# A two-block transformer kernel on one core: first stream in pieces, product quarters ahead of attention's first macro, a finer wait in the state-space output, one ones matmul for each norm

## What is computed

```python
h = x
h = h + nsa_mixer(rmsnorm(h), ...)      # 16 heads: compressed, selected and window attention, gated
h = h + s5_mixer(rmsnorm(h), ...)       # state space, GLU with gelu, output product
h = rmsnorm(h, final_norm)
h = h + even_mixer(rmsnorm(h), ...)     # stick-breaking attention beside retention
h = h + conv_ffn(rmsnorm(h), ...)
h = h + odd_mixer(rmsnorm(h), ...)      # gated linear attention, gates from log_sigmoid, chunks of 64
h = h + conv_ffn(rmsnorm(h), ...)
```

## Time and profile before

| | |
|---|---|
| median of 3 runs | 1942.9 us (1942.57 to 1943.28) |
| the profiled execution | 1942.15 us, its span 1940.3 us |
| PE busy | 1916.4 us, 99% of the span |
| DVE, ACT, POOL busy | 1144.0, 578.4 and 795.3 us |
| the chain that ended last, by engine | PE 89%, DVE 8%, waits for nothing visible 1%, ACT 1%, DMA 1% |
| DMA | 167.72 MB, mean 86 GB/s |
| TensorE clock granted, mean | 0.997 |

### The profile page before, as it was taken

How to read it: one execution, slowest core, us unless ns; L and a number is a source line. 1 busy time by engine, 2 the same in 40 slices (tenths; PEclk the granted TensorE clock), 3 DMA queues, 4 the chain that set the end, 5 groups by cost and what they waited for, 6 DMA issues and landing times.

```text
span 1940.3 us, 26524 instructions
## 1 busy us (share of the span) xinstructions
PE 1916.4 (99%) x9866; PEld 1517.6 (78%) x9866; DVE 1144.0 (59%) x2079; ACT 578.4 (30%) x1118; POOL 795.3 (41%) x454
## 2 busy tenths in 40 slices
PE   8999999999999999999999999999999999999999
PEld 5967777788788776777688888888788888888887
DVE  5769998788975545766664444333654454445311
ACT  3126566416641134454221111101322221111000
POOL 3532222368754432222244444444233334444443
PEclk9999999999999999999999999999999999999999
DMA  5621111223123231121132222232112222222332
GB/s 185 186 76 34 44 34 34 77 84 112 34 68 102 92 125 55 55 66 65 61 109 97 97 97 97 98 109 98 65 66 77 76 99 92 95 96 97 110 118 76
DMA packets 54628, 167.72 MB, mean 86 GB/s; under 512 B 6864, under 2 KB 14928, under 8 KB 54144
## 3 DMA queue, kind: packets, MB, share of 16 engines
q1 hardware_dynamic: 46624, 155.21, 23.8%
q10 hardware_dynamic: 7904, 11.16, 2.1%
HBM read 157.96 MB, written 2.10 MB: 82 GB/s over the span
## 4 chain that ended last, share of the span: by engine, by line
PE 89%; DVE 8%; issue 1%; ACT 1%; DMA 1%; ACTq 0%; POOL 0%; DVEq 0%
PE bank L186 18%; PE bank L187 17%; PE bank L190 17%; PE bank L587 5%; PE bank L592 5%; PE bank L588 5%; DVE prob L1656 2%; DVE ssb L1643 2%; PE bank L1278 1%; PE bank L200 1%; PE bank L206 1%; PE bank L1303 1%; PE bank L203 1%; PE bank L2634 1%; PE bank L2623 1%
## 5 line engine op out<-in xcount | busy, mean ns | idle before, releaser
L169 POOL TENSOR_TENSOR wlo<-raw,whi 128x1024 fp32r<-128x1024 f32 x248 | 594.8, 2398 | 895.5 <-DVE whi L177 895.5
L177 DVE CAST whi<-raw 128x1024 fp32r<-128x1024 f32 x288 | 206.4, 717 | 338.4 <-PE bank L190 240.9
L186 PE MATMUL bank<-xh,whi 128*128 128x512 f32 x888 | 347.1, 391 | 0.0
L187 PE MATMUL bank<-xl,whi 128*128 128x512 f32 x888 | 345.6, 389 | 0.0
L190 PE MATMUL bank<-xh,wlo 128*128 128x512 f32 x888 | 219.4, 389 | 0.0
L186 PEld LDWEIGHTS bank<-xh,whi 128*128 128x128 f32 x888 | 166.7, 188 | 37.6 <-issue 3.1
L187 PEld LDWEIGHTS bank<-xl,whi 128*128 128x128 f32 x888 | 166.7, 188 | 34.9 <-issue 0.5
L190 PEld LDWEIGHTS bank<-xh,wlo 128*128 128x128 f32 x888 | 166.7, 188 | 34.7
L587 PE MATMUL bank<-xh,whi 128*128 128x512 f32 x424 | 175.3, 414 | 1.4 <-DVE whi L177 1.4
L588 PE MATMUL bank<-xl,whi 128*128 128x512 f32 x424 | 166.0, 392 | 0.0
L186 PE MATMUL bank<-ghi,whi 128*128 128x512 f32 x308 | 119.8, 389 | 0.0
(11 more groups left out here) (431 smaller groups left out, 3477.6 us busy)
## 6 DMA issues: line engine op xcount, KB each, us to landing
raw<-in_weights_dram SPq DMA_DIRECT2D x288, 512.0 KB, 3.2
h<-in_x_dram SPq DMA_DIRECT2D x2, 1024.0 KB, 7.2
out_dram<-h ACTq DMA_DIRECT2D x8, 256.0 KB, 2.0
etab<-in_even_tables_dram ACTq DMA_DIRECT2D x1, 1730.0 KB, 6.5
sz<-su SPq DMA_DIRECT2D x16, 64.0 KB, 2.0
sz<-su SPq DMA_DIRECT2D x16, 48.0 KB, 2.0
x_kh<-kvc_h ACTq DMA_DIRECT2D x2, 256.0 KB, 5.0
x_kl<-kvc_l ACTq DMA_DIRECT2D x2, 256.0 KB, 6.9
```

The costliest lines, as they stand in the source:

```text
L169: nc.gpsimd.tensor_tensor(wlo[:, s % 2, :], raw[:, s, :], whi[:, s % 2, :].bitcast(F32), ALU.subtract).then_inc(w_lo, 1)
L177: nc.vector.tensor_copy(whi[:, t_of_4 % 2, :], raw[:, t_of_4, :]).then_inc(w_hi, 1)
L186: nc.tensor.matmul(to, w_h[k], rhs_hi(k), start=first and k == 0, stop=False)
L187: nc.tensor.matmul(to, w_h[k], rhs_lo(k), start=False, stop=False)
```

## The change

Six edits. (1) At the start SP asks for `x` in four pieces of two chunks, with the first weight tile between the second and the third, and takes over `nsa_loads` from ACT. ACT issues the gains first, then `wgate`, `tables` and `par`; it starts on the first pieces when gains and piece are there, and its waits for `tables` stand where they are first used. PE runs three instead of four matmuls on zeros, all of the first four gate matmuls before tile 0 and the rest in pairs at chunks 4 and 6 of it, and the sum over squares moves from chunk 3 to chunk 0 of the second tile. DVE leaves its `par` arithmetic (`s5_exponent`, `s5_fraction`, 11 small instructions) until the squares are summed, and `s5_step` (7) until after tile 0. (2) The eighth square is added to `ssq` by DVE as well, and each norm has one ones matmul. (3) Three quarters of a product tile, (0, 0), (0, 1) and (1, 0) in `AHEAD`, move from macros 0 and 1 to places ahead of macro 0. (4) `s5_out`'s first two tiles wait for one count less of `acc_free`. (5) In `dve_odd` the query half of `dve_decayed(0)` stands ahead of the fourth head's gates. (6) The counters `n_pe` and `n_cc` are merged into `n_kvl` and `n_cb`, with the same waits.

```diff
@@ -119,7 +119,10 @@
         def sp_stream(sp):
-            sp.dma_start(raw[:, 0, :], A["weights"][0]).then_inc(w_landed[0], 16)
-            for half in range(2):
-                sp.dma_start(h[:, 4 * half:4 * half + 4, :], A["x"][:, 4 * half:4 * half + 4, :]).then_inc(x_landed[half], 16)
+            for pair in range(KC // 2):
+                if pair == 2:
+                    sp.dma_start(raw[:, 0, :], A["weights"][0]).then_inc(w_landed[0], 16)
+                two = slice(2 * pair, 2 * pair + 2)
+                sp.dma_start(h[:, two, :], A["x"][:, two, :]).then_inc(x_landed[pair], 16)
             for t in range(1, RING):
                 sp.dma_start(raw[:, t, :], A["weights"][t]).then_inc(w_landed[t], 16)
+            nsa_loads(sp)
             first = T0["s5_in"] + KC if "s5_in" in names else TILES
...
@@ -226,3 +229,3 @@
 
-        SQ, SM, SS = 8, 6, 2
+        SQ, SM, SS = 8, 7, 1
         splitting = [n for n in range(len(norms)) if norms[n] != N_FINAL]
...
@@ -261,3 +264,4 @@
                 dve.wait_ge(sq_sum, SMB[n] + m - 1)
-            nc.vector.tensor_tensor(ssq[:], ssq[:], bank[5 + m % 2][:], ALU.add).then_inc(sq_sum, 1)
+            square = sq[:, 1, :] if m == KC - 1 else bank[5 + m % 2]
+            nc.vector.tensor_tensor(ssq[:], ssq[:], square, ALU.add).then_inc(sq_sum, 1)
 
...
@@ -268,5 +272,3 @@
             pe.wait_ge(sq_sum, SMB[n] + SM)
-            nc.tensor.matmul(ssum[:], ones, ssq[:], start=True, stop=False).then_inc(ss_done, 1)
-            pe.wait_ge(sq_ready, SQB[n] + SQ)
-            nc.tensor.matmul(ssum[:], ones, sq[:, 1, :], start=False, stop=True).then_inc(ss_done, 1)
+            nc.tensor.matmul(ssum[:], ones, ssq[:], start=True, stop=True).then_inc(ss_done, 1)
 
...
@@ -280,3 +282,4 @@
 
-            act.preload_act_table_set(LOG_EXP)
+            if n:
+                act.preload_act_table_set(LOG_EXP)
             act.wait_ge(ss_done, SSB[n + 1])
...
@@ -347,3 +350,3 @@
 
-        def pe_residual(pe, stage, n, hi_ready, lo_ready, per=1, rhs=None, chunks=(KC,)):
+        def pe_residual(pe, stage, n, hi_ready, lo_ready, per=1, rhs=None, chunks=(KC,), spare=0):
 
...
@@ -356,3 +359,3 @@
                     if q == 0:
-                        pe.wait_ge(acc_free[m % 2], (o0 + m) // 2 + 1)
+                        pe.wait_ge(acc_free[m % 2], (o0 + m) // 2 + (0 if m < spare else 1))
                     tile = (t0 + m * per + q + 1, (m * per + q) % 2, acc[m % 2][:], *rhs[q], chunks[q], q == 0, q == per - 1)
...
@@ -388,2 +391,4 @@
                     dve_unscaled_low(dve, n, m - 1)
+            if n is not None:
+                dve_square_sum(dve, n, KC - 1)
             if n in UNSCALED:
...
@@ -1117,10 +1120,10 @@
 
-        def nsa_loads(act):
+        def nsa_loads(sp):
             for to, what in ((ntab, "nsa_tables"), (w2, "w2"), (pe_in, "pe"), (sd, "s5_d")):
-                act.dma_start(to[:], A[what]).then_inc(n_loaded, 16)
+                sp.dma_start(to[:], A[what]).then_inc(n_loaded, 16)
 
         def pe_nsa(pe):
-            def gates(first):
-                pe.wait_ge(x_landed[first // 4], 16)
-                for m in range(first, first + 4):
+            def gates(pair):
+                pe.wait_ge(x_landed[pair], 32 if pair == 0 else 16)
+                for m in (2 * pair, 2 * pair + 1):
                     nc.tensor.matmul(bank[2][0:48, :], wgate[:, m, :], h[:, m, :], start=m == 0, stop=m == KC - 1)
...
@@ -1129,3 +1132,3 @@
             pe.wait_ge(acc_free[1], 1)
-            for _ in range(4):
+            for _ in range(3):
                 nc.tensor.matmul(acc[1][:], xf[:, 0, 0:P], xf[:, 0, :], start=True, stop=True)
...
@@ -1135,6 +1138,8 @@
                     gates(0)
+                    gates(1)
                 def beside(k):
-                    if u == 0 and k == 4:
-                        gates(4)
-                    if u == 1 and k == 3:
+                    if u == 0 and k in (4, 6):
+                        gates(k // 2)
+                    if u == 1 and k == 0:
+                        pe.wait_ge(loaded, 16)
                         pe_squares(pe, 0)
...
@@ -1188,3 +1193,4 @@
             mm.then_inc(n_c2, 1)
-            pe.wait_ge(n_cc, 4)
+            pe_beside(pe, 0, 0)
+            pe.wait_ge(n_cb, 4 + 4)
             pe.wait_ge(acc_free[0], freed(O0["nsa_rest"] + 4))
...
@@ -1192,2 +1198,4 @@
             pe_scores(pe, 0)
+            pe_beside(pe, 0, 1)
+            pe_beside(pe, 1, 0)
             pe_cmp_turn(pe, 0, bank[7])
...
@@ -1322,3 +1332,4 @@
             pe_turn(pe, M, 0)
-            pe_beside(pe, M, 0)
+            if (M, 0) not in AHEAD:
+                pe_beside(pe, M, 0)
             pe_turn(pe, M, 1)
...
@@ -1331,3 +1342,4 @@
                 pe_cmp_turn(pe, i + 1, bank[3])
-            pe_beside(pe, M, 1)
+            if (M, 1) not in AHEAD:
+                pe_beside(pe, M, 1)
             if m == 0:
...
@@ -1342,5 +1354,2 @@
 
-            act_s5_pow2(act)
-            act.wait_ge(loaded, 32)
-
             def high(m):
...
@@ -1349,13 +1358,14 @@
 
-            act.wait_ge(x_landed[0], 16)
-            for m in range(4):
-                high(m)
-            for m in range(3):
-                act_square(act, 0, m)
-            act.wait_ge(x_landed[1], 16)
-            for m in range(4, KC):
-                high(m)
-            for m in range(3, KC):
+            act.preload_act_table_set(LOG_EXP)
+            for pair in range(KC // 2):
+                act.wait_ge(x_landed[pair], 32 if pair == 0 else 16)
+                for m in (2 * pair, 2 * pair + 1):
+                    high(m)
+                if pair in (1, 2):
+                    act_square(act, 0, pair - 1)
+            for m in range(2, KC):
                 act_square(act, 0, m)
+            act.wait_ge(loaded, 16)
             act_rstd(act, 0)
+            act_s5_pow2(act)
 
...
@@ -1511,5 +1521,3 @@
 
-            s5_exponent(dve)
-            s5_fraction(dve)
-            dve.wait_ge(loaded, 32)
+            dve.wait_ge(x_landed[0], 32)
             dve.wait_ge(n_wgate, 16)
...
@@ -1517,13 +1525,12 @@
                                     ALU.mult).then_inc(n_wgate, 1)
-            split_tile(dve, 0, 0)
-            for m in range(4):
+            for m in range(KC):
                 dve_unscaled_low(dve, 0, m)
+                if m == 1:
+                    split_tile(dve, 0, 0)
             dve_square_sum(dve, 0, 1)
-            dve_square_sum(dve, 0, 2)
-            for m in range(4, KC):
-                dve_unscaled_low(dve, 0, m)
             split_tile(dve, 1, 0)
-            for m in range(3, KC - 1):
+            for m in range(2, KC):
                 dve_square_sum(dve, 0, m)
-            s5_step(dve)
+            s5_exponent(dve)
+            s5_fraction(dve)
 
...
@@ -2032,2 +2039,6 @@
             dve_odd_split(dve, "q", i)
+
+        def dve_decayed_key(dve, i):
+
+            t = T0["odd_in"] + odd_tile("q", i)
             dve.wait_ge(tile_done, t + 2)
...
@@ -2048,4 +2059,5 @@
             dve_alpha(dve, 2)
+            dve_decayed_query(dve, 0)
             dve_alpha(dve, 3)
-            dve_decayed(dve, 0)
+            dve_decayed_key(dve, 0)
             for i in range(4):
...
@@ -2412,2 +2425,3 @@
             if u == 0:
+                s5_step(dve)
                 s5_exponential(dve)
...
@@ -2695,3 +2709,3 @@
                         KC, True, True).then_inc(tile_done, 1)
-            pe_residual(pe, "s5_out", None, lambda k: pe.wait_ge(s_oh, k + 1), lambda k: pe.wait_ge(s_ol, k + 1), rhs=[(lambda k: gh[:, k, :], lambda k: gl[:, k, :])])
+            pe_residual(pe, "s5_out", None, lambda k: pe.wait_ge(s_oh, k + 1), lambda k: pe.wait_ge(s_ol, k + 1), rhs=[(lambda k: gh[:, k, :], lambda k: gl[:, k, :])], spare=2)
 
...
@@ -2878,6 +2893,6 @@
         def _(act):
-            s5_early_loads(act)
-            act.dma_start(gains[:], A["gains"]).then_inc(loaded, 16)
+            act.dma_start(gains[:], A["gains"]).then_inc(x_landed[0], 16)
             act.dma_start(wgate[:], A["wgate"]).then_inc(n_wgate, 16)
             act.dma_start(tables[:], A["tables"]).then_inc(loaded, 16)
+            s5_early_loads(act)
             for key, name in blocks:
```

More of the change, by code:

```diff
@@ L105, in build @@
         loaded = sem("loaded")
-        x_landed = [sem("x_landed0"), sem("x_landed1")]
+        x_landed = [sem(f"x_landed{pair}") for pair in range(KC // 2)]
         sq_ready = sem("sq_ready")
@@ L1085, in build @@
         n_zero = sem("n_zero")
-        n_pe = sem("n_pe")
         n_kvh = sem("n_kvh")
@@ L1092, in build @@
         n_c2 = sem("n_c2")
-        n_cc = sem("n_cc")
         n_dist = sem("n_dist")
@@ L1153, in pe_nsa @@
             pe.wait_ge(n_x2, 16 * 16)
-            pe.wait_ge(n_pe, 4)
+            pe.wait_ge(n_kvl, 8)
             pe.wait_ge(n_gs, 2)
@@ L1202, in nsa_tile @@
             return (4 + 2 * i + 1, m) if m < 2 else None
+        AHEAD = ((0, 0), (0, 1), (1, 0))
         def pe_beside(pe, M, half):
```

(16 more changed lines are left out.)

## The result

The changed kernel takes 1929.74 us in the median of 4 runs (1929.67 to 1929.93), the kernel before 1942.74 (4 runs beside it, 1942.17 to 1943.28). The ratio is 0.9935, with a 95% interval of 0.9923 to 0.9947: 13.0 us faster. The profiled execution's span is 1927.9 us against 1940.3, so the two traces account for 12.4 of it.

The account below looks back on a forecast made before the run. PE, busy for 99% of the span, was taken as the bound. Terms 7.8 + 3.4 + 0.7 + 1.5 + 0.1 = 13.5 us gave 1928.65 for the profiled execution, 1929.4 for the median; 8-in-10 range 1927.0 to 1932.8.

Parts of the forecast that it names:

- The wait of 1 us: Ahead of the second tile's first ones matmul: PE arrives at about 20.1 and waits for DVE's sums until 21.05.
- Start: Program start to third tile: earlier gains and `wgate` let it begin at 27.4 against 35.15; 7.8 us, bounds 6.1 to 9.0.
- case (e): First tiles: clock stays at 1.2 GHz as PE starts sooner but waits at each chunk; slower, about 1947 us; 4%.
- Case (a): Start: ACT's small rows served first, `wgate` lands at 5.5, start gives 9 us; 1928.2 us, or 1927; 7%.
- What is late next: Copies for the compression, behind DVE's cast for tile 3: landing at 60.3, wanted by PE at 60.4, just in time.
- Attention's beginning: Ahead of macro 0: moved quarters fill PE's waits and keep the clock full; 3.4 us, set by DVE, bounds 2.0 to 4.1.
- Norms: Five later norms: one 0.85 us matmul less, but waits for DVE's sum, loss at joined norms; 0.7 us, bounds 0.2 to 4.2.
- State-space output: State-space output: finer wait starts PE at 646.9 instead of 648.36, then `gh` and `gl` limit; 1.5 us, bounds 1.2 to 1.55.
- Gated linear attention: Query split 3 us earlier, but PE waits for a subtraction slowed beside POOL; 0.1 us, bounds -0.3 to 1.4.
- The 13.5 of the sum: Whole kernel: 7.8 + 3.4 + 0.7 + 1.5 + 0.1 us saved, forecast at 62%.

Follow-up runs that it names:

- the last run: Changed kernel with eighth sum earlier, ones matmul later, cast behind the fourth subtraction, and the first norm's ones matmul back at the second tile's fourth chunk: 1924.84 us.
- (alone): Kernel before with only the three product quarters moved ahead of attention's first macro: 1938.54 us, ratio 0.9980.
- the filler: Kernel before with three unread f32 matmuls ahead of the transposes of the compressed probabilities, no quarter moved: 1940.24 us, ratio 0.9992.
- the start-alone run: Kernel before with only the start's edit and the merged counters, two ones matmuls in every norm: 1936.05 us, ratio 0.9971.

## Why the prediction was right, point by point

The forecast of 1929.4 us lies 0.3 from the measured 1929.7, and most of the mechanisms were found in the trace. Two terms were off in size, the start and the norms. Attention's term was right in size, but the clock has a larger part in it than I gave it. The wait of 1 us that I put at the end of the start wasn't there. That the total is so close is partly luck, as the end of this section says.

- **Start, 7.8 predicted, 7.14 measured.** `wgate` landed at 6.99 instead of 6.7, DVE's chain then went as worked out (the fourth chunk took 2.88 us), the eighth sum ended at 21.44 instead of 21.05, and the third tile began at 28.01 instead of 27.4. Of the 0.66 us that are missing 0.3 are `wgate`, 0.1 is DVE's chain, 0.1 the restart (PE begins 0.15 us behind the end of a sum that it waits for, not 0.05), and 0.13 the ones matmul with the tile behind it (6.42 us for 6.29). PE's side was wrong: I had it at the second tile at 20.1 with 1 us to wait, and it got there at 21.42, level with DVE. It began the gates 0.4 late, and from the fourth chunk on its first tile took 8.33 us instead of 7.5; each change between gate matmuls and products costs 0.1 to 0.2 us there (0.52 us from the last gate matmul to the next product, where gate matmuls stand 0.43 apart), and the sum had nothing for it. So the start was bound by both engines. The clock stayed at full, and the run without zero matmuls shows what that is worth, 2.5 us; case (e), a kernel at half clock, needed just this to go wrong. Case (a), `wgate` by 5.5, didn't come: it landed 5.8 us after its issue at 1.19, beside the transfers of `x`. That case was also what a rule of the Trainium skill (DMA: Bandwidth & Descriptors, on arbitration) pointed to; the landing speaks against it, while the order of packets is shown by no run here.
- **What is late next.** The copies held, by 0.3 us where I had worked out 0.1, and the last run shows that this is a real limit: PE waits 0.5 us for them as soon as DVE's reading of the first tile slips by 1.4.
- **Attention's beginning, 3.4 predicted, 3.55 and 3.4 (alone) measured.** The steps came as described: no wait for `cpr` over 0.5 us, scores of macro 2 at 130.79, the first copy of macro 1 at 132.76. Before, these stood at 141.49 and 143.46, so 10.7 sooner, of which 7.1 are the start's. I had some 1.2 us of half clock only in the upper bound; the filler shows that some 1.5 of the term are the clock's: DVE's work, which I took to decide the term, comes sooner when PE isn't at half clock.
- **Norms, 0.7 predicted, 0.2 measured.** This is the mis-sized term. The wait came where it was predicted, 0.65 us, and so did the loss at the joined norms (-0.64 for -0.55) and the gain of 0.86. But at three norms I took 0.85 saved less 0.7 waited. The traces give 1.31 us from the first ones matmul to the next `xl` product before (410.44 to 411.75) and 0.53 after (400.55 to 401.08), so 0.78 saved, and 0.81 from PE's readiness (399.74, the old start less the lead) to its start. It comes to nothing at each of the three. Moving the sum or the ones matmul removes the wait and gives 2.7 to 3.4 us, so the theory that PE waits for DVE's order of work, and not for the number of matmuls, is shown.
- **State-space output, 1.5 predicted, 1.44 measured**: it starts 1.6 sooner and gives a little back at the last chunk, as forecast.
- **Gated linear attention, 0.1 predicted, 0.15 measured**: the subtraction took 2.33 us beside `wlo`, and 0.69 with the cast moved behind it. The rule of the Trainium skill (SBUF — State Buffer, "SBUF: two separate sides"), that a DVE operation with two SBUF inputs and a GpSimd operation that reads SBUF lock each other out, fits both rows: beside POOL the subtraction ended at 1368.23, 0.54 us behind the end of `wlo`. The edit's own idea was worth 1.5 us; the place of the cast took it away.

The medians differ by 13.0 and the spans by 12.4 us. The 13.5 of the sum was 1.1 too high against the traces; the median of before that the forecast started from lay 0.75 above its profiled execution, that of the changed kernel only 0.07, and this, which is luck, hid most of it.

## What to carry to other kernels

When an engine waits for a sum, look first at what stands ahead of the sum in the other engine's program: leaving out a 0.85 us matmul gave nothing at three norms, while moving an addition ahead of a chunk that no one wanted yet, or the matmul behind work that was ready, gave 0.7 to 0.9 at each. Before moving anything, check in the rows that the wait is there: at the first norm it was 0.2 us, and the move that was to save 0.7 gave nothing. Filling the gap on TensorE with useful work paid twice here, for the gap and for the clock behind it; price the second by a filler that does nothing. And an edit that lets POOL begin sooner can lengthen the two-input DVE operation that PE waits for.

## What the runs showed of the hardware beyond that

- The same start of the program regains the clock at different moments: in six profiled executions the first product tile began between 17.43 and 19.05 us, with a mean granted clock in the window from 10.7 to 17.5 of 0.75 in the two where it began before 18 us, and of 0.50 to 0.57 in the other four. The runs of before spread over 2.3 us; those of the changed kernel, which never falls to half clock there, over 0.3.
- The column of the granted clock reads 1.00 at the start of a program while matmuls run at half speed: without the zero matmuls the windows say

```profile
7.20:10.70 3.50, 2.72 (x4) 0.80 (x5) 3.50 (x6) 2.24 (x5) 0.97 (x1) 1.00 1.04 415
10.70:17.50 6.80, 6.80 (x17) 2.47 (x16) 6.80 (x8) 3.27 (x6) 2.32 (x2) 1.00 0.95 376
```

  and the gate matmuls in them took 6.52 us for 3.63. The trace has its first record of the clock, a full one, only at 13.84 us in this execution, and the column counts a stretch without a record as 1.00. Up to there the gate matmuls' records stand 0.85 us apart, behind it 0.43. In the kernel before and in the changed one the first record stands at 7.28 and 7.70, and the zero matmuls ahead of it are 0.86 us apart; in the start-alone run it stands at 4.56, and the zero matmuls go from 0.86 to 0.43 us apart there. So every program here started at half clock, and the zero matmuls brought the full clock forward by 6 us (7.70 for 13.84).
- Three f32 matmuls whose result nobody reads, put where PE would stand idle, made the kernel 1.5 us faster by its landmarks, though the interval of its medians (0.9982 to 1.0001) can't tell it from none.
